# Fourteen context expert rows moved from between the score searches to between the filter tiles, with their gathers on four shared buffers

## What is computed

```python
s = einsum('thpd,phkd->thpk', q, peer_keys)          # 8 heads, two halves, 128 keys
sv, si = top_k(s, 16)                                # the score searches
...                                                  # the best 16 pairs per head: 128 experts a token
act = gelu(einsum('cd,ced->ce', xc, u_tab[ic])) * gc # u rows: one dot product each
out = einsum('ced->cd', act, v_tab[ic])              # v rows: one weighted sum each
```

## Time and profile before

| | |
|---|---|
| median of 3 runs | 2613.67 us (2603.48 to 2614.12) |
| the profiled execution | 2599.84 us, of it 2598.0 us span, 1.84 us around it |
| PE busy | 2357.6 us, 91% of the span |
| DVE busy | 1773.5 us, 68% |
| POOL busy | 962.0 us, 37% |
| ACT busy | 493.8 us, 19% |
| transfers | 647 MB, 249 GB/s on average |
| chain that ended last | PE 63%, DVE 15%, DMA 9%, issue 7%, ACT 4% |

### The profile page before, as it was taken

The page is one execution under the profiler, slowest core; times in us unless marked ns, Lnnn a source line. Parts: engine busy times, 40 slices in busy tenths (PEclk is TensorE's granted clock), DMA queues, the critical chain, the costliest instruction groups (busy, mean ns, idle before and its releaser), DMA issues.

```text
span 2598.0 us, 43625 instructions
## 1 busy us (share of the span) xinstructions
PE 2357.6 (91%) x18034; PEld 1660.0 (64%) x18034; DVE 1773.5 (68%) x3472; ACT 493.8 (19%) x994; POOL 962.0 (37%) x774
## 2 busy tenths in 40 slices
PE   6999969788888879997899799999999999998997
PEld 3555538577777764443488677776776677775664
DVE  2111362256677766675899886799899898875767
ACT  2111225234434421101112211000001000100101
POOL 0000000000355450543620005666665677774753
PEclk9999979889999988998999679999999999999998
DMA  8340130310566661867883028999999999999997
GB/s 323 141 167 37 64 122 3 122 42 14 176 225 205 208 223 41 320 243 257 324 315 123 18 70 319 368 395 381 408 406 353 409 409 405 388 401 412 409 409 305
DMA packets 163935, 647.01 MB, mean 249 GB/s; under 512 B 21062, under 2 KB 21958, under 8 KB 158298
## 3 DMA queue, kind: packets, MB, share of 16 engines
q0 software_dynamic: 110592, 402.70, 41.0%
q1 hardware_dynamic: 53146, 241.52, 24.0%
HBM read 635.50 MB, written 8.65 MB: 248 GB/s over the span
## 4 chain that ended last, share of the span: by engine, by line
PE 63%; DVE 15%; DMA 9%; issue 7%; ACT 4%; POOL 2%; another core or an unknown queue 1%; SPq 0%; DVEq 0%; POOLq 0%; ACTq 0%
PE ps L1094 9%; DMA arena<-in_peer_v,arena 8%; PE ps L1105 8%; PE ps L610 6%; PE ps L1116 5%; PE ps L1070 4%; PE ps L866 4%; DVE arena L2101 3%; PE ps L1010 2%; PE ps L977 2%; PE ps L1035 2%; POOL arena L2278 2%; PE ps L1020 2%; PE ps L614 2%; PE ps L834 1%
## 5 line engine op out<-in xcount | busy, mean ns | idle before, releaser
L1105 PE MATMUL ps<-arena 128*128 128x512 f32 x1024 | 465.6, 598 | 23.6 <-DVE arena L2140 23.3
L1094 PE MATMUL ps<-arena 128*128 128x256 f32 x2048 | 481.0, 389 | 0.0
L2278 POOL DMA_INDIRECT arena<-in_peer_u,arena x256 | 345.4, 1349 | 347.8 <-DVE arena L1894 193.0
L1094 PEld LDWEIGHTS ps<-arena 128*128 128x128 f32 x2048 | 392.9, 195 | 69.4 <-issue 19.6
L2278 POOL DMA_INDIRECT arena<-in_peer_v,arena x256 | 303.4, 1185 | 199.0 <-DVE arena L2101 131.9
L2101 DVE SCALAR_TENSOR_TENSOR arena<-arena 128x1024 f32<-128x1024 f32 x252 | 315.1, 1283 | 82.0 <-DMA arena<-in_peer_v,arena 75.3
L2266 POOL DMA_INDIRECT arena<-in_peer_u,arena x128 | 167.6, 1309 | 549.2 <-DVE arena L1894 317.7
L1105 PEld LDWEIGHTS ps<-arena 128*128 128x128 f32 x1024 | 194.3, 191 | 223.0 <-issue 208.7
L2096 DVE SCALAR_TENSOR_TENSOR arena<-arena 128x1024 bf16<-128x1024 f32 x256 | 303.0, 1221 | 31.1 <-DMA arena<-in_peer_u,arena 29.8
L1116 PEld LDWEIGHTS ps<-arena 128*128 128x128 bf16 x3072 | 206.3, 156 | 69.3 <-issue 47.2
L1116 PE MATMUL ps<-arena 128*128 128x32 bf16 x3072 | 209.2, 243 | 23.0 <-DVE arena L2133 22.4
(11 more groups left out here) (361 smaller groups left out, 3273.6 us busy)
## 6 DMA issues: line engine op xcount, KB each, us to landing
arena<-in_uT SPq DMA_DIRECT2D x128, 512.0 KB
arena<-in_peer_v SPq DMA_DIRECT2D x128, 512.0 KB
arena<-in_w_ada SPq DMA_DIRECT2D x12, 2048.0 KB, 21.7
arena<-in_peer_wq SPq DMA_DIRECT2D x12, 2048.0 KB, 9.5
arena<-in_w_in SPq DMA_DIRECT2D x6, 2048.0 KB, 7.5
arena<-in_w_out SPq DMA_DIRECT2D x4, 2048.0 KB, 7.6
arena<-in_peer_u,arena POOLq DMA_INDIRECT x384
arena<-in_peer_v,arena POOLq DMA_INDIRECT x384
```

Source lines behind the costliest of these rows:

```text
L1094: m = pe.matmul(ps[:, 4 + i % 2, 0:ND], us[i % UB][:, k, :], hTd[:, k, :], start=(k == 0), stop=(k == KD - 1))
L1105: m = pe.matmul(ps[:, 2 * r + c, :], sgel[:, i % SBUFS, P * r:P * r + P], vs[i % VB][:, 512 * c:512 * c + 512], start=(i == 0), stop=(i == ...
L2278: pool.indirect_dma_start(gring[:, n % RING, :], None, a[("peer_u", "peer_v")[e]][0], bass.IndirectOffsetOnAxis(ap=ids[:, t, m:m + 1], axi ...
```

## The change

Fourteen rows are asked for earlier: 2 behind the last unit, 1 behind each of the first four filter tiles, 2 behind each of the second four. As many fewer stand between the searches: 1 behind each of the first four and none behind the others. Everything between keeps its number of rows, so there each is a row 14 further on. Rows 126 to 139 take the four common buffers in turn, and the ring of eight starts at row 140; row 238 is still the first of the last ring of four. POOL's wait for the gate moves from row 126 to row 140. The Gelu between u and v rows moves on ACT ahead of the first spectra copy, since row 128 is now asked for among the first filter tiles.

```diff
-WIDE_FROM, WIDE_TO = 126, 238
+RING_TO, WIDE_FROM, WIDE_TO = 126, 140, 238
...
-        k = n % (CR + EXTRA) if n < WIDE_FROM else (n - WIDE_FROM) % slots if n < WIDE_TO else (n - WIDE_TO) % CR
+        k = (n % (CR + EXTRA) if n < RING_TO else (n - RING_TO) % CR if n < WIDE_FROM else (n - WIDE_FROM) % slots if n < WIDE_TO
+             else (n - WIDE_TO) % CR)
...
-            sp.wait_ge(S("c_used"), WIDE_FROM - 1)
+            sp.wait_ge(S("c_used"), RING_TO - 1)
...
+            act.wait_ge(S("c_used"), SLOTS)
+            A(dots_c, dots_c, ACT.Gelu).then_inc(S("gelu_ok"), 1)
             ng = 2
             for o in range(2):
                 for k in range(NLT):
...
                 if o == 0:
                     mix_out(0)
-                    act.wait_ge(S("c_used"), SLOTS)
-                    A(dots_c, dots_c, ACT.Gelu).then_inc(S("gelu_ok"), 1)
...
-                    slot, dst = (gring_u if c < WIDE_FROM else gring_c)[k], acc_c[c % 2]
+                    slot, dst = (gring_u if c < RING_TO else gring_c)[k], acc_c[c % 2]
...
+            rows_c(2)
             own.settle()
             nf, nu, ni = 2, 2, 2
             for j in range(NLT):
                 dve.wait_ge(S("hf_mm"), nf + 1)
                 filter_tile(0, ...)
                 nf += 1
+                rows_c(1)
             own.settle()
             group_norm(1, NT)
             for j in range(NLT):
                 dve.wait_ge(S("hf_mm"), nf + 1)
                 filter_tile(1, ...)
                 nf += 1
+                rows_c(2)
             rows_c(20)
...
-                rows_c(2 if r < 2 else 1)
+                rows_c(1 if r < 4 else 0)
...
-                pool.indirect_dma_start((gring_u if n < WIDE_FROM else gring_c)[k], None, a[("peer_u", "peer_v")[e]][0],
+                pool.indirect_dma_start((gring_u if n < RING_TO else gring_c)[k], None, a[("peer_u", "peer_v")[e]][0],
```

## The result

The changed kernel took 2635.59 us (median of 9 runs, 2615.82 to 2644.68); nine runs of the kernel before, taken with it, 2604.02 us (2596.02 to 2614.12). The ratio is 1.0105, 95% interval 1.0082 to 1.0128: **slower by about 1%**. The forecast of 2619.1 (range 2603 to 2630, "same" 0.75) was wrong: 2635.59 lies above the range. One execution of e8 took 3107 us and is left out of its ratio.

The account below looks back on a forecast made before the run. The prediction took the stage touched to be bound by PE, with DVE counting only where PE waits for it. Terms 6.0 + 3.3 + 0.9 - 1.3 - 3.5 = +5.4 us gave 2619.1 us on the median, range 2603 to 2630.

Parts of the forecast that it names:

- the term on the searches: Searches: fourteen rows leave for 0 us; delay from the ring of four behind the second norm would be caught up.
- Second filters: Second filters: six of eight added rows stand ahead of the last tile and delay PE, less idle time, +6.0 us.
- a sign of being wrong: Filters: the prediction said it is wrong if DVE waits for gathers inside them.
- PE's clock: Spectra of the second filters: PE restarts at a lower clock after a gap, +3.3 us, bounds 0 and 3.3.
- Rows behind the loads: Behind the second filters: 19 rows instead of 13 follow the loads, DVE late at the fourth product, +0.9 us, bounds 0 to 7.7.
- Table load: Later root on ACT: with Gelu ahead of the first root one table load goes, -1.3 us, bounds 0 and -1.35.
- ACT's stop: Queries: ACT's 10.87 us wait, read as late instructions, shrinks with fewer gathers in flight, -3.5 us, bounds 0 and -7.0.
- First six rows: Behind the last unit and in the first filters: six rows fit into DVE's idle gaps, cost 0.
- Searches worth 0: Searches: without the rows DVE just waits for PE, so 17.8 us less DVE work gains 0.
- A: Second filters: the ring of four starves, DVE stands 6.8 us more with PE behind it, 2629.4 us; chance 0.15.
- B: Searches are on the path after all, DVE's 17.8 us come through to the gates, some 2599 us; chance 0.10.
- C: Loss doesn't arrive: ACT's stop goes wholly and PE's clock holds, or the last stage absorbs it, some 2612; chance 0.20.

Follow-up runs that it names:

- e8: Kernel before with only six rows moved, from behind the second filters to behind the last unit and among the first filter tiles: 2603.36 us, 1.0021.
- e1: Changed kernel with the ring of eight extended to row 251, so the 18 rows behind the second norm have eight buffers: 2564.39 us, 1.0057.
- e2: Kernel before, no row moved, with the last ring of four starting at row 224 instead of 238: 2568.96 us, 1.0069.
- e13: The changed kernel, unaltered, timed again in the fourth set: 2630.77 us, 1.0099.
- e14: Changed kernel with the ring of eight up to row 251 (e1's kernel), timed beside e13: 2626.12 us, 1.0088.
- e7: Changed kernel with 14 rows instead of 20 behind the second filters, six back between the searches, ring of eight to row 245: 2608.62 us, 1.0019.
- e3: Changed kernel with only six of the fourteen rows moved, none in the second filters, ring of eight from row 132 to 243: 2554.92 us, 1.0016.
- e15: e8's order with the ring of eight up to row 243, so the last ring of four starts at row 244 instead of 238: 2609.37 us, 1.0023.
- e12: The kernel before, unaltered, run for a profile in the third set: 2545.97 us.
- e9: e8's kernel with one wait added: POOL issues row 126 only when row 124 has been used: 2554.57 us, 1.0026.

## Why the prediction was wrong

**The step that failed** is one sentence of the term on the searches: "Rows 238 and on now run in the ring of four behind the second norm. Even 20 us more there would be caught up: DVE gains 1.1 us a step on PE and has about 20 us before the Exp." The 20 us came (20.4). They were not caught up. I compared DVE with its last deadline, the Exp, and left out the near one: with four score buffers ACT's fifth copy of these scores waits for the first search, so DVE may be late by four scores, 4 x 3.90 = 15.6 us, counted from the first copy at 1328.06, and not until the Exp some 100 us later. DVE's first search ended 31 us behind that copy, and 15.13 us of ACT's time and 12.18 of PE's went. With PE's slow restart the stage took 14.6 us over its bare 125.2. The term stood at 0 and measured +14.6. e1 takes this away and e2 makes it alone, both in a prompt set; in the sets in which the change itself was timed, the traces show it, and the total only weakly (e13 against e14). After it DVE did wait longer for the Exp, 9.05 us where I had said about 10: that part of the argument held and was of no use.

**Second filters, +6.0: right.** Measured +7.4: the same rows, plus 1.63 us for a gather, which the prediction had named as a sign of being wrong. **PE's clock, +3.3: right in kind**, measured +2.2 (granted clock 0.51 for the first 5 us of the spectra). Its cause was not the long gap: the clock was at 0.53 already on the fourth tile, before the gap, and at full speed 4.5 us after the restart. e7, which keeps the eight rows, has 16.6 and 31.6 us there, e8 without them 9.1 and 28.9; the two totals do not tell them apart (1.0019 and 1.0021).

**Rows behind the loads, +0.9: mis-sized**, measured +5.5 in the first transform. The -1.2 in the inverse is not a part of it given back: e7 and e8, whose transform takes the 31.6 us of before, have an inverse of 30.2 as well. It is the clock, which behind the same wait of 3.90 us stood at 0.66 over the first 5 us and not at 0.50. The bound of 7.7 held it. I took the wait for the first late gather from before (6.09 us), but it grew to 11.48 us, since DVE now comes to that gather sooner after the loads are issued: 1072.4 (loads), 1088.88 (used). Rows ahead of a load had covered its flight; 13 of 20 rows behind it leave cover, 19 leave none. e3 (18 rows, none in the second filters) shows +4.8, e7 (13 rows) zero.

**Table load, -1.3: right**, -1.1. The rule of the Trainium skill ("ScalarE: Activation LUTs", What ACT_TABLE_LOAD costs) would have given 2.7 with its drain; nothing of a drain came back.

**ACT's stop, -3.5: mis-sized**, -7.7 in the changed kernel, where it is gone in all three profiles. But it is no property of a kernel alone: in one kind of set it comes in before (twice), in e14 and e15, in a harmless form in e7 and e8, and in the other kind in none. My reading, which no run proves: where a starved DVE stops the stage anyway, late instructions find the time to arrive.

**First six rows, 0: right** as to the filters (16.4 in both), open as to the last unit: 59.2 us there against 55.6. In such sets the kernels that gather early took 54.5 to 61.0 in seven profiles and before 55.4 and 55.6; in prompt sets it is 43.3 to 46.3 against 42.8 to 45.7, no difference. With one profile each this is no more than a suspicion of 3 to 5 us.

**Searches worth 0: right.** Four kernels with fewer rows in them stand at the same 125.22 us as before does in e12.

**The rivals.** A had the right resource, four buffers against the time of a gather, at the wrong place: in the second filters it cost 1.63 us and not 6.8, because gathers there took 6.5 us; behind the second norm it decided. B was wrong. C's mechanism for the stop came true and was outweighed. The sum with the measured sizes: 7.4 + 2.2 + 5.5 - 1.2 - 1.1 - 0.7 + 6.9 = +19.0; 3.6 in the last unit and -2.6 behind the scores make it about 20, where the three ratios give 22 to 27. Of what the forecast missed, the ring less the stop is the largest located part, 14.6 - 7.7 = +6.9 where -3.5 was put; the rows behind the loads are the next, +5.5 for +0.9.

**What stays open:** the last unit, and the rest of 2 to 7 us between the sum and the ratios; whether e8's order costs anything in the sets that are not prompt; why the clock stays low half as long in the inverse of some runs; and how the ring's price divides between its four buffers and its place.

## What to carry to other kernels

When rows move from sparse to dense places, set the number of buffers times the time between two uses against the flight of one gather at that place: four buffers were enough at 4.07 us a row and starved at 1.28. Look at the place too, where one ring hands over to another: at the same 4.07 us a row DVE waited 0.8 us in before, where the ring of four starts on buffers long free, but 9.8 and 8.8 us in e8 and e9, where its first buffer had been used two rows before. Test a delayed engine against its nearest ring, not against its last deadline: a ring of four results lets it be late by four results and no more. And rows that stand ahead of a large load are cover for its flight; moving them up moves that cover away.

## What the runs showed of the hardware

**Two kinds of sets.** The kernel before took 2604.4 and 2602.8 us on two sets and 2550.5 and 2548.2 on the two others, 2% less, with every run of a set on its side. The third and the fourth set carry the same chip number, 0, and were taken within a quarter of an hour, yet they are of different kinds; if the number names one chip, this is a matter of the session and not of the chip. The profiles differ in waits that have no releaser in the program. View of the waits, kernel before in its first profile (total us, times, longest):

```profile
ACT arena L1432 <- remote: 41.4, 7, 8.2
...
ACT arena L1333 <- remote: 28.4, 5, 5.7
...
DVE arena L1985 <- remote: 27.5, 5, 5.5
ACT arena L1321 <- remote: 26.7, 4, 14.9
...
ACT arena L1258 <- remote: 25.3, 5, 5.1
...
ACT arena L1401 <- remote: 10.9, 1, 10.9
```

Three lines of the scan (L1333, L1985, L1258) wait about 5 us each, five times in the ten units; L1321 has longer ones, and L1432 lies in the dense pass. All such waits together are 34 and 189 us in this profile; in e12 and e1 there is none, and a unit with rows takes about 48 us instead of 53. The stop in the queries belongs to the same family. I read them as instructions that arrive late behind gathers (a packet of the instruction queue lies beside the stop); no run proves it. The Trainium skill ("Runtime: NRT & Kernel Launch", Instruction fetch mechanics) calls sequential fetch mostly hidden; the prompt sets agree, with no such wait, and the others would not, if that reading is right.

The consequence for a comparison was not expected either: the same edit had another price in each kind. The ring of four costs the score stage 14 us over its bare 125.2, but only 6.9 over the 132.9 of before, since it takes the place of a stop. e1's kernel stood at 1.0057 and 1.0049 in prompt sets and at 1.0088 in the other, for another reason: e14 has the same stop as before, and loses its further 9 us in the last unit (60.2 against 55.4 us), on the way from the first to the second filters (53.1 against 49.7) and in the projection (74.2 against 72.9). Why there is not shown.

**The clock behind one and the same wait.** Ahead of the first inverse PE waits 3.90 us in every run. Over the same 5 us the granted clock was 0.50 in before and e12, and the inverse took 31.5 us; it was 0.66 in after, e7 and e8, and the inverse took 30.2. So a wait of this length was followed by more or less of the lower level (1.2 of 2.4 GHz), at a difference of 1.2 us.

**A gather behind large transfers.** The same 512 KB gather took 6.5 us in the second filters, 5.3 and 6.8 in front of the searches, 14.9 behind a 2 MB load and a 2 MB write, and the first one behind the 5 MB of loads was used 16.5 us after these were issued.
